# Decoder layer: GpSimd takes the low parts of the first pairs' weights and of two combinations of x from VectorE

## The reference

```python
def modulate(h, shift, scale):
    return h * (1 + scale[:, None, :]) + shift[:, None, :]

def swiglu(h, w_gate, w_up, w_down):
    return (jax.nn.silu(h @ w_gate) * (h @ w_up)) @ w_down

def reference(x, c, ...):
    ...
        h = modulate(rms_norm(x, g_ffn1[l]), sh1, sc1)
        x = x + 0.5 * ga1[:, None, :] * swiglu(h, w_gate1[l], w_up1[l], w_down1[l])
        h = modulate(rms_norm(x, g_mix[l]), sh2, sc2)
        y = hybrid_mixer(h, positions, w_in[l], b_forget[l], ...)
        x = x + ga2[:, None, :] * y
        h = modulate(rms_norm(x, g_ffn2[l]), sh3, sc3)
        x = x + 0.5 * ga3[:, None, :] * swiglu(h, w_gate2[l], w_up2[l], w_down2[l])
    return rms_norm(x, g_final)
```

## Time and profile before

| | |
|---|---|
| median of 3 runs | 2234.31 us |
| the profiled execution | 2234.3 us |
| its span | 2232.6 us |
| TensorE busy | 2202.2 us (99%), 10472 matmuls |
| VectorE busy | 1559.5 us (70%) |
| ScalarE busy | 1071.6 us (48%) |
| GpSimd busy | 903.2 us (40%) |
| mean granted TensorE clock | 0.996 |

### The profile page before, as it was taken

One profiled execution on the slowest core, in us unless ns is written; L12 is line 12 of the kernel. 1 busy time (PEld: TensorE's weight loads), 2 busy tenths in 40 slices (PEclk: granted clock), 3 DMA queues, 4 the chain that ended last, 5 costly groups with the idle time before them and its releaser, 6 DMA issues.

```text
span 2232.6 us, 29463 instructions
## 1 busy us (share of the span) xinstructions
PE 2202.2 (99%) x10472; PEld 1814.6 (81%) x10472; DVE 1559.5 (70%) x2116; ACT 1071.6 (48%) x2028; POOL 903.2 (40%) x782
## 2 busy tenths in 40 slices
PE   7999999999999999999999999999999999999998
PEld 6888888888887888888787887888778888888887
DVE  7976767578878757732899998578785454547765
ACT  5533333333454553344899898425443333333344
POOL 0044555400122655544557656447205555530013
PEclk9999999999999999999999999999999999999999
DMA  7156565374561533444814065323223222347454
GB/s 281 73 194 221 210 216 202 137 295 165 188 224 50 162 125 137 152 166 141 226 53 119 15 161 152 120 95 142 104 87 126 89 106 103 109 162 262 148 177 160
DMA packets 152033, 338.01 MB, mean 151 GB/s; under 512 B 14224, under 2 KB 36880, under 8 KB 151888
## 3 DMA queue, kind: packets, MB, share of 16 engines
q1 hardware_dynamic: 150624, 333.57, 44.3%
q10 hardware_dynamic: 1264, 2.56, 0.5%
HBM read 247.28 MB, written 86.64 MB: 150 GB/s over the span
## 4 chain that ended last, share of the span: by engine, by line
PE 82%; DVE 11%; ACT 3%; issue 2%; DMA 1%; POOL 1%; SPq 0%; DVEq 0%; ACTq 0%; POOLq 0%
PE ps L3184 11%; PE ps L3185 11%; PE ps L3186 11%; PE ps L3332 6%; PE ps L3330 6%; PE ps L3331 6%; PE ps L3411 4%; PE ps L3413 4%; PE ps L3412 4%; PE ps L3538 3%; PE ps L3563 2%; PE ps L3564 2%; PE ps L3523 2%; PE ps L3142 2%; PE ps L3144 2%
## 5 line engine op out<-in xcount | busy, mean ns | idle before, releaser
L3184 PE MATMUL ps<-r_main,r_z 128*128 128x512 f32 x1232 | 482.0, 391 | 6.1 <-DVE r_main L2212 3.4
L1964 POOL TENSOR_TENSOR r_z<-f_main,r_z 128x512 fp32r<-128x512 f32 x213 | 304.6, 1432 | 446.6 <-ACT r_z L1231 446.6
L3185 PE MATMUL ps<-r_main,r_z 128*128 128x512 f32 x1232 | 480.3, 390 | 0.0
L3186 PE MATMUL ps<-r_main,r_z 128*128 128x512 f32 x1232 | 480.3, 390 | 0.0
L1231 ACT CAST r_z<-f_main 128x512 fp32r<-128x512 f32 x254 | 155.8, 621 | 346.7 <-PE ps L3186 277.5
L3184 PEld LDWEIGHTS ps<-r_main,r_z 128*128 128x128 f32 x1232 | 231.9, 188 | 60.2 <-DVE r_main L2212 4.4
L3186 PEld LDWEIGHTS ps<-r_main,r_z 128*128 128x128 f32 x1232 | 231.8, 188 | 48.2
L3185 PEld LDWEIGHTS ps<-r_main,r_z 128*128 128x128 f32 x1232 | 231.8, 188 | 47.6 <-issue 0.2
L3330 PE MATMUL ps<-r_main 128*128 128x512 f32 x604 | 235.8, 390 | 0.0
L3332 PE MATMUL ps<-r_main 128*128 128x512 f32 x604 | 235.0, 389 | 0.0
L3331 PE MATMUL ps<-r_main 128*128 128x512 f32 x604 | 235.0, 389 | 0.0
(11 more groups left out here) (385 smaller groups left out, 4497.7 us busy)
## 6 DMA issues: line engine op xcount, KB each, us to landing
act_d<-f_main SPq DMA_DIRECT2D x154, 256.0 KB, 2.0
f_main<-act_d SPq DMA_DIRECT2D x70, 512.0 KB, 4.9
f_main<-in_ada SPq DMA_DIRECT2D x56, 512.0 KB, 5.2
f_main<-in_wg SPq DMA_DIRECT2D x20, 1024.0 KB, 5.0
f_main<-in_wu SPq DMA_DIRECT2D x20, 1024.0 KB, 5.0
f_w<-in_wo SPq DMA_DIRECT2D x40, 512.0 KB, 4.0
f_main<-in_wmix SPq DMA_DIRECT2D x18, 1024.0 KB, 5.4
f_e<-in_we SPq DMA_DIRECT2D x10, 1024.0 KB, 5.6
```

Source lines behind the costliest of these rows:

```text
L1964: pool.tensor_tensor(prod_lo_t[slot], source_of(g), prod_hi_t[slot].bitcast(F32), ALU.subtract).then_inc(s["wl"], 1)
L3184: pe.matmul(out, wh, hi, start=start, stop=False, skip_group_check=True)
L3185: pe.matmul(out, wh, lo, start=False, stop=False, skip_group_check=True)
L3186: return pe.matmul(out, wl, hi, start=False, stop=stop, skip_group_check=True)
```

## The change

It moves subtractions from VectorE's list to GpSimd's. No operation is added or dropped. In the two feed-forward blocks GpSimd makes the low parts of the weights of products 8 to 27 (in the list the combination 7 of pair 1's two halves is 12 and 13). It also makes the low parts of combinations 6 and 4 of x, after weight products 14 and 21. In the mixer it makes those of combinations 6 and 4 after products 2 and 5. These low parts of x are counted on `s_added` instead of `nsem["hl"]`, so all waits on them go through two new helpers. On VectorE one `taken` moves ahead of a sum of weights, and in the mixer the four t4 stand in a row.

```diff
-HL, HH = (0, 32, 64), (0, 32, 64)
+HL, HH = (0, 24, 48), (0, 32, 64)
+X_POOL = (6, 4)
+X_AFTER = {14: 6, 21: 4}
...
+        def x_split(engine, k, q, i):
+
+            if q in X_POOL:
+                engine.wait_ge(s_added, 3 + 8 * k + 4 * X_POOL.index(q) + i + 1)
+            else:
+                engine.wait_ge(nsem["hl"], HL[k] + (20 + i + 1 if q == 5 else x_count(q, i, k)))
+
+        def x_all_split(engine, k):
+
+            engine.wait_ge(nsem["hl"], HL[k] + 24)
+            engine.wait_ge(s_added, 3 + 8 * k + 8)
...
+            def x_low(k, q):
+
+                for i in range(4):
+                    pool.wait_ge(nsem["hh"], HH[k] + x_count(q, i, k))
+                    pool.tensor_tensor(x_lo[k][q][:, i], chunk(q, i), x_hi[k][q][:, i].bitcast(F32), ALU.subtract).then_inc(s_added, 1)
...
-            pool.wait_ge(fsem[0]["wl"], fbase[0]["wl"] + SECOND + 6)
-            for g in range(SECOND + 6, N_PROD):
+            pool.wait_ge(fsem[0]["wl"], fbase[0]["wl"] + PRELUDE)
+            for g in range(PRELUDE, N_PROD):
                 weight_low(0, g)
+                if g in X_AFTER:
+                    x_low(0, X_AFTER[g])
...
             for g in range(M_PROD):
                 mix_weight_low(g)
+                if g in (2, 5):
+                    x_low(1, {2: 6, 5: 4}[g])
...
-            for g in range(PRELUDE):
+            for g in range(N_PROD):
                 weight_low(1, g)
-            pool.wait_ge(fsem[1]["wl"], fbase[1]["wl"] + SECOND + 6)
-            for g in range(SECOND + 6, N_PROD):
-                weight_low(1, g)
+                if g in X_AFTER:
+                    x_low(2, X_AFTER[g])
...
                     if p == 0:
-                        dve.wait_ge(nsem["hl"], HL[2 * f] + 4 * len(X_ORDER))
+                        x_all_split(dve, 2 * f)
...
                     if m >= 12:
                         t1_t3(k, m - 12)
-                        if k == 0:
-                            weight_low(f, m - 4)
...
-                for g in range(8, 12) if k == 2 else ():
-                    weight_low(f, g)
                 for i in range(4):
                     x_low(k, 7, i)
-                weight_low(f, 12)
                 weight_sum(f, 1, UP, 3)
...
-                weight_low(f, 13)
-                weight_low(f, 14)
-                for i in range(4):
-                    x_low(k, 6, i)
                 weight_sum(f, 1, UP, 2)
-                weight_low(f, 15)
-                weight_low(f, 16)
                 x_low(k, 5, 0)
...
                 for i in range(4):
                     t4(k, i)
-                x_low(k, 4, 0)
-                x_low(k, 4, 1)
                 plain_taken(f, 2)
-                x_low(k, 4, 2)
                 plain_taken(f, 3)
-                x_low(k, 4, 3)
...
-                for q in (6, 5):
-                    for i in range(4):
-                        x_low(1, q, i)
+                for i in range(4):
+                    x_low(1, 5, i)
                 mix_taken(2)
                 mix_sum(0, 4)
-                for i in range(5):
-                    if i < 4:
-                        t4(1, i)
-                    if i > 0:
-                        x_low(1, 4, i - 1)
+                for i in range(4):
+                    t4(1, i)
                 mix_taken(4)
```

More of the change, by code:

```diff
@@ L567, in build @@
         s_x_top = sem("x_top")
-        s_added = sem("x_squares_added")
+        s_added = sem("x_parts_on_pool")
         s_ada = [sem(f"ada_in{r}") for r in range(8)]
@@ L859, in gate_up_loads @@
                         if p == 2:
-                            sp.wait_ge(nsem["hl"], HL[k] + 4 * len(X_ORDER))
+                            x_all_split(sp, k)
                         for m in range(4):
@@ L1494, in mix_taken @@
                     if u == 0 and j >= 2:
-                        act.wait_ge(nsem["hl"], HL[1] + x_count(4, j))
+                        x_split(act, 1, 4, j)
                     elif u > 0 and j != 1:
@@ L2220, in t1_t3 @@
                 b11, b12, b22 = chunk(5, i), chunk(7, i), chunk(3, i)
-                dve.wait_ge(s["hl"], HL[k] + x_count(3, i, k))
+                x_split(dve, k, 3, i)
                 if i == 0:
@@ L2230, in t2 @@
                 dve.wait_ge(s["t"], x_sum_at(k, 3, i))
-                dve.wait_ge(s["hl"], HL[k] + x_count(7, i))
+                x_split(dve, k, 7, i)
                 dve.scalar_tensor_tensor(chunk(6, i), chunk(3, i), shift_of(k, 3, i), chunk(5, i), ALU.add, ALU.subtract).then_inc(s["t"], 1)
@@ L2400, in first_pair @@
                 x_low(k, 5, 3)
-                weight_low(f, 17)
                 taken(f, AT[1, UP, 6])
                 weight_sum(f, 1, GATE, 4)
-                weight_low(f, 18)
                 weight_sum(f, 1, UP, 4)
-                weight_low(f, 19)
                 taken(f, AT[1, GATE, 5])
-                weight_low(f, 20)
-                weight_low(f, 21)
                 taken(f, AT[1, UP, 5])
@@ L2422, in first_pair @@
                     act_sum(f, 0, i)
-                weight_low(f, 22)
+                taken(f, AT[1, UP, 2])
                 weight_sum(f, 2, GATE, 2)
-                weight_low(f, 23)
-                taken(f, AT[1, UP, 2])
                 last_quarter(f, 1)
-                for g in (24, 25, 26):
-                    weight_low(f, g)
                 taken(f, AT[1, UP, 4])
                 weight_sum(f, 2, GATE, 4)
-                weight_low(f, 27)
                 taken(f, AT[1, UP, 3])
@@ L3246, in gate_up @@
                         for i in range(4):
-                            pe.wait_ge(nsem["hl"], HL[k] + x_count(q, i, k))
+                            x_split(pe, k, q, i)
                             for r in range(2):
@@ L3353, in mix_plain @@
                     for i in range(4):
-                        pe.wait_ge(nsem["hl"], HL[1] + x_count(q, i))
+                        x_split(pe, 1, q, i)
                         for e in range(3):
@@ L3408, in mix @@
                         if u == 0:
-                            pe.wait_ge(nsem["hl"], HL[1] + x_count(q, k))
+                            x_split(pe, 1, q, k)
                         wh, wl = m_hi3[slot][:, k], m_lo3[slot][:, k]
```

## The result

| | before | after |
|---|---|---|
| median | 2234.35 us (4 runs, 2233.33 to 2234.53) | 2253.81 us (4 runs, 2253.45 to 2254.16) |
| ratio | | 1.0089, 95% interval 1.0073 to 1.0105 |
| profiled execution, span | 2234.3, 2232.6 us | 2253.45, 2251.6 us |
| VectorE busy, instructions | 1559.5 us | 1561.2 us, 64 instructions fewer |
| GpSimd busy | 903.2 us | 1001.3 us |

The account below looks back on a forecast made before the run. TensorE, busy 2202.2 of 2232.6 us, was taken as the bound, so only its idle time could be won; losses of 7.8 + 4.5 + 6.1 = 18.4 us on 2234.3 gave 2252 us, range 2246 to 2258 (2240 to 2261 with C and D).

Parts of the forecast that it names:

- The price of a pair: One VectorE operation with two SBUF inputs plus one GpSimd subtraction, taking turns: about 1.75 us, at worst 1.97.
- Rival D: Slower by more: a pair costs the full 1.97 us, 30 pairs add 6.6 us, 2259 us; chance 0.11.
- Block 0 to product 15: First feed-forward block: late low parts make product 15 start at 98.1 in place of 94.14, 4.0 us lost.
- Block 0 to product 24: First feed-forward block: product 24 starts at 129.7 in place of 121.88 us, 7.8 us lost.
- the chain of act_sum, SiLU and seed copy: Block 0 behind product 20: two sums and one act_sum pair with low 22 and 23; product 24 starts at 129.7.
- Block 1: Second feed-forward block: product 15 2.3 us late, product 24 at 1677.8 in place of 1671.73, 6.1 us lost.
- Mixer: Low parts of combinations 5 and 4 end later; product 6 starts at 727.8 in place of 723.23, 4.5 us lost.
- Hidden parts: Pair 2's weight loads move from 104 to 109 us, wanted only at 116; the new counter costs no instruction.
- Rival C: Slower by half: VectorE keeps its turn, GpSimd gets in only in gaps; 10 us in all, 2244; chance 0.2.
- Rival A: Faster: the engines' turns cost nothing on the path, VectorE's subtractions go to an idle engine; 2231 us; chance 0.08.
- Rival B: No change: fewer lost pairs, meeting only slack; gains and losses both near 3 us, 2235; chance 0.06.

Follow-up runs that it names:

- e3_after_one_input: The changed kernel, with VectorE's t1 to t4, sums and low parts of x replaced by same-size operations with one SBUF input; 2231.22 us (0.9988).

## Why the prediction was right

- **The price of a pair** (1.75 us, bounds 1.29 and 1.97) held: 1.70 from start to start at 84.79, 86.49 and 88.19, with a median duration of 1732 ns for the 24 low parts of x. Rival D, full exclusion at 1.97 and 2259, fell, and with it the estimate by the Trainium skill's rule: the rule names the right pairs of operations, but a pair costs less than the sum of the two.
- **Block 0 to product 15** (98.1): 97.70. The sum in `s3` at 83.29 (83.4 forecast), low 13 done at 86.5 (86.6), combination 6 at 95.0 (95.35). That TensorE waits here for low 15 rather than for combination 6 is what the list said. Product 14 itself lost some 0.5 us, where I had about 2: TensorE reached it 1.08 us later than I took it to, so more of the four pieces were there. That changed only where the time was lost, since low 15 sets product 15.
- **Block 0 to product 24** (129.7): 130.19. Combination 4 ended at 117.1 (117.3), and product 21 starts 6.60 late (6.9 forecast at the end of product 20). From there another 1.71 us go to product 24, where I had 0.9, and 0.24 more to product 28: the chain of act_sum, SiLU and seed copy was mis-sized. Two of the four act_sum met low 22 and low 23 (117.09 and 118.77), where I had counted one. So this first link took 4.90 us at 117.60, for 2.74 before, and ScalarE's SiLU waited for it:

```profile
121.14 0.60 ACT L1277 ACTIVATE f_main<-ps 128x512 f32<-128x512 f32 x1 [4.42 <-DVE f_main L2295]
```

- **Block 1** (6.1): 7.0, the same step. Product 21 is 5.1 late (5.0), and the chain takes another 1.71 us to product 24, where I had 1.1, and 1.94 to product 28. Its links are the same as in block 0 (act_sum 4.92 us for four), and products 22 and 23 wait for the SiLU, 1.04 and 1.24 us:

```profile
1682.28 0.47 PE L3178 MATMUL ps<-r_main,r_z 128*128 128x512 f32 x1 [1.04 <-ACT f_main L1277]
...
1686.51 0.47 PE L3178 MATMUL ps<-r_main,r_z 128*128 128x512 f32 x1 [1.24 <-ACT f_main L1277]
```

- **Mixer** (4.5): 3.8 at product 6, 3.9 at product 12. The steps stand in the forecast order, counted from product 0 (8.60 us late): VectorE's low parts of combination 5 from 710.06 to 716.4 (716.6), combination 4 done at 725.75 (726.4), product 6 at 727.05 (727.8). The term that was too large is what the four low parts of combination 5 and the pairs of combination 4 cost: a pair is 1.70 from start to start, and some met less than a whole piece. The mark that I set, product 6 some 12 us late in all, came out at 12.42:

```profile
718.66 6.31 DVE L2238 TENSOR_TENSOR r_main<-f_main,r_main 128x512 fp32r<-128x512 f32 x4 [3.00 <-ACT r_main L1234]
724.89 0.69 DVE L2665 TENSOR_TENSOR ps<-ps,f_main 128x512 f32<-128x512 f32 x1
```

- **Hidden parts** stayed hidden: no wait on the loads of pair 2's weights or on the new counter shows among TensorE's waits, and products 8 to 14 of block 1 keep their distance (12.06 us late throughout).
- **One mark was wrong in size.** I expected TensorE's waits on low parts of x to be 1 us each; they are 13, none over 0.8. The large ones (1.7) are on low 15, behind them.
- **Rival C**, VectorE keeps its turn, fell: four t2 took 6.89 us, so the turns alternate. **Rival A** (which counts all 28 moved subtractions in VectorE's 44 us, where 22 lie) gave 2231 for a kernel without turns, and with turns taken away the change measured 2231.22; but so did the kernel before, 2230.72. So the turns were the price, and the move had nothing to win either way. **Rival B**, no change, fell with the 19.5 us.

The parts missed by +0.8, -0.6 and +0.9 us; the sum, 19.5 for 18.4, by 1.1. That the sum is so close owes something to luck: the mixer's term, too large, offset part of the chain in the two blocks. The 0.45 us that come back ahead of block 1 were not in the forecast at all.

## What to carry to other kernels

A low share of busy time on GpSimd is no free capacity: ask first which of its operands and of VectorE's lie in SBUF, and price a moved piece at what it adds to its neighbour (1.1 us here) against what it saves (0.6). Look for the neighbours on both sides: what waits for the moved piece, and what the slowed engine still has to deliver. Where an engine is full at a place, a few exchanges in the lists (3 us here, 0.9 to 4.9 by the interval, no work moved) can be worth more than an offload, but follow the chain one wait further than the one that you remove.

## What the runs showed of the hardware

- The smallest operation pays the full turn. A TENSOR_TENSOR over 128x4 took 0.15 us before and 1.27 when it came 0.05 us after the start of a GpSimd piece of 1.30 (68.18 and 68.13 above), and 1.26 in the run without other turns. The Trainium skill ("SBUF — State Buffer", "SBUF: two separate sides") says that the one that starts first keeps the shared ports for its whole instruction and the other is blocked; this row agrees.
- A pair that alternates costs 1.70 us from start to start, less than 1.29 + 0.68, and less than the sum of the 1.26 and 0.60 that the two need from start to start when alone. Why, no run here tells.
- TENSOR_REDUCE over an axis of length one, from SBUF to SBUF, takes 0.59 to 0.60 us from start to start for 128x512 float32, as TENSOR_TENSOR does (0.60), and isn't disturbed by GpSimd: the 241 of them that overlap in time with a GpSimd piece in `e3_after_one_input` have a mean of 678 ns and a greatest of 687.
